# Four rearrangements in a hybrid recurrent layer: the gate rows, the way into the gated DeltaNet, the matrix memory's sample and the last products

## Chip, cores and metric

The kernel runs on one core of a Trainium2 chip. Its measure is the device time of one execution in microseconds.

## What is computed

One layer (D_MODEL = 1024) over a prompt of 1024 tokens and, at the same time, 8 sequences of 4 tokens each (the sample) that continue from given states. Three token mixers work on one input projection and are merged through gates; a feed-forward block and a final norm follow. The reference, cut:

```python
def mixer(xn, p, st):
    proj = jnp.einsum('btd,dc->btc', xn, p['w_in']).astype(f32)
    ...
    h, C1, n1, m1 = mlstm_scan(heads(ml_q), heads(ml_k) * HEAD_DIM ** -0.5, heads(ml_v), i_log, f_log, C0, n0, m0)
    ...
    conv = jax.nn.silu(sum(buf[:, j:j + t_len] * cw[j] for j in range(CONV_W)))
    o_gd, S1_gd = gdn_scan(l2n(heads(cq)) * HEAD_DIM ** -0.5, l2n(heads(ck)), heads(cv), beta, logg, S0_gd)
    y_gd = unheads(head_rms(o_gd) * p['gd_norm_w']) * jax.nn.silu(gd_z)
    ...
    o_hg, S1_hg = hgrn_scan(heads(jax.nn.silu(hg_q)), heads(k_hg), heads(hg_i), heads(jnp.log(g_f)), S0_hg)
    ...
    br = jnp.einsum('btnw,nwd->btnd', ys, p['w_branch'])
    merged = jnp.sum(gates * br, 2)
    return jnp.einsum('btd,de->bte', merged, p['w_out']), states

x = x + mixer(rmsnorm(x, norm1_w))
x = x + jnp.square(jax.nn.relu(rmsnorm(x, norm2_w) @ w_up)) @ w_down
y = rmsnorm(x, final_norm_w)
```

## The kernel before

All dense products (input projection, merge, output projection, feed-forward) have one form. A tile is 128 output columns over all T = 1056 tokens (1024 of the prompt, 32 of the sample), in three groups of 352 tokens (`TG`, `GN`). Each float32 operand is split in a high and a low part, and `dense` (line 415) makes three matmuls for each of the 8 pieces of the contraction: high by high, low by high, high by low. All of them have line 432 in the profile. Weights come through SyncE (`load_w`, line 384) into `w_raw`; ScalarE copies the high part (`make_hi`, `w_hi`, line 406), GpSimd subtracts it for the low part (`make_lo`, `w_lo`, line 412). Each group accumulates in one of two banks, `D0` and `D1`. ScalarE copies it out, into `u_in` for the columns of the short convolution (line 507) or into `stage` (line 451), from where it stores whole tiles to `proj` in memory (line 458). A group can begin only when ScalarE has emptied its bank.

The mixers' small operations lie between dense groups, in an order written out by hand. Each mixer's function is called once for each engine and calls `slot()` at fixed places. A `Filler` holds a list of weights, one for each slot, and puts that share of a run of tiles there: the dense pieces on TensorE, on ScalarE the weights' high parts and the copies of finished groups, on GpSimd the low parts. Each engine does its list strictly in order. On ScalarE and GpSimd a slot's work is held back until the next `slot()` or `slot.evacuate()`.

The four places, in order of time:

- **The gate rows** (`rows`, with the tiles 2 and 3 in its slots). The input and forget gates, decays and their running sums are made as rows of 36 x 128 by a long chain of small operations on VectorE, with exponentials on ScalarE and four tiny transposes on TensorE (`ends`, `prev`, `tok`). `tok` is the table with a column for each chunk.
- **The way into the gated DeltaNet.** After the convolutions GpSimd inverts small triangular blocks (`b_t`; VectorE turns them into `b_tt`). SyncE stores both to `td` (line 716) and loads them back in another shape as `d_t` and `d_tt` (line 1705). The chunk's product at line 1949 on TensorE needs all eight of these loads. `d_z` holds the output gate of a chunk; its columns are the last tiles before the loop (`stored_all(eng, GD0)` waits until they are in memory). `d_bc` are the four gate rows of a chunk, spread over all partitions; VectorE needs the next chunk's at the end of a chunk (`d_de`, line 1569), and ScalarE's four exponentials (line 1580) need that.
- **The matrix memory's sample** (`mlstm` with `sample`). Four heads read the states (line 2253), then come the denominators (2265, 2266), the sums of the keys (2270), the first of four state updates (`states("kv", h)`, line 872, two matmuls of 32 x 512), the transposes of `m_oc` (2276), and, with dense pieces between them, the other three updates.
- **The last products** (`last_down`): the down projection of the last block in three groups of 8 pieces of output `d`, the final norm's sum of squares (`SUM3`, shown as `f_sum`), and the scaling of finished columns (`SCALED` says which are scaled behind which piece).

Of the kernel before, what the change touches and what calls it, by code (L numbers as in the profile page):

```python
# [9 lines left out]
ALU = mybir.AluOpType  # L10
# [87 lines left out]
class Tile:  # L98
# [8 lines left out]
    @property  # L107
    def slot(self):
        return self.base % 2
# [15 lines left out]
def build(nc, xT, w_proj, w_half, w_full, par, con, rowpar, segrow, m0, conv0, st_ml, st_mn, st_gd, st_hg,  # L125
# [6 lines left out]
    with ExitStack() as ctx:  # L132
# [682 lines left out]
        hs_pool = steps("hs_pool", "gw" + DECAY_STEPS)  # L815
        GX_SLOTS, HS_SLOTS, MX_SLOTS = 15, 9, 10
        lb_dve, lb_act = steps("lb_dve", "d r n lb om"), steps("lb_act", "e ln")

        def pcols(tile, ntile, col, n):

            v = proj[tile:tile + ntile].rearrange("t p c -> p t c")
            return v[:, :, bass.ds(col, n)]
# [547 lines left out]
        def rows(kind, eng, slot):  # L1370
# [16 lines left out]
            if kind == "dve":  # L1387
# [38 lines left out]
                scan("loc", r_l[:, :], r_a[:, 1, :], r_in[:, 0, :], MASKED, ALU.add, ALU.max)  # L1426
                slot()

                eng.wait_ge(*rw_pe.after("ends"))
# [36 lines left out]
                slot()  # L1466
            if kind == "act":
                eng.wait_ge(*rw_dve.after("bc"))
                eng.activation(r_b[:, :, :], r_a[:, 0:2, :], ACT.Exp, scale=-1.0).then_inc(*rw_act.step("e"))
# [18 lines left out]
                eng.dma_start(s_m, r_mo[RP:RP + H, :]).then_inc(rw_mo, 16)  # L1488
                slot()
                eng.wait_ge(*rw_pe.after("tok"))  # L1490
                by_q = M[0][:, 0:5 * (RP + H)].rearrange("p (q x) -> p q x", q=5)
# [5 lines left out]
            if kind == "pool":  # L1497
                for _ in range(4):
                    slot()
            if kind == "pe":  # L1500
                slot()
                eng.wait_ge(*rw_dve.after("loc"))
                eng.transpose(M[1][0:1, 0:RP], r_a[0:RP, 0, last:CH], ident[0:RP, 0:RP])
                eng.transpose(M[1][0:1, RP:2 * RP], r_l[0:RP, last:CH], ident[0:RP, 0:RP]).then_inc(*rw_pe.step("ends"))
                slot()
                eng.wait_ge(*rw_dve.after("mp"))
                eng.transpose(M[2][0:RP, 0:1], r_c[0:1, 3 * RP:4 * RP], ident[0:1, 0:1]).then_inc(*rw_pe.step("prev"))
                slot()
                eng.wait_ge(*rw_dve.after("kd2"))
                eng.wait_ge(*rw_act.after("ex2"))  # L1510
                for q in range(5):
                    i = eng.transpose(M[0][:, q * (RP + H):(q + 1) * (RP + H)], r_tok[q], ident[0:RP + H, 0:RP + H])
                i.then_inc(*rw_pe.step("tok"))
                slot()
# [83 lines left out]
        def gdn(kind, eng, n, slot, sample, with_next=False, between=None):  # L1598
# [9 lines left out]
            def hn(x, o=0):  # L1608
                return x[:, o:o + C4].rearrange("p (h n) -> p h n", n=N)
# [48 lines left out]
            if kind == "sp":  # L1658
# [8 lines left out]
                if between != "rest":  # L1667
                    for k in range(2):
                        eng.dma_start(hn(B.qk, k * C4), pcols(GD_TILE + 4 * (1 - k), 4, col0, N)).then_inc(gx_in if sample else gd_in, 16)

# [5 lines left out]
                if n is None and not sample:  # L1676
# [3 lines left out]
                    for s_ in cv_st:  # L1680
                        eng.wait_ge(s_, 16 * NCONV // 2)
                eng.dma_start(hn(B.v), pcols(GD_TILE + 8, 4, col0, N)).then_inc(gx_in if sample else gd_in, 16)
                if n is not None or sample:
                    prefetch(eng, None if sample else n, (gd_dve, "ge"))
                    token_rows()

                def gates():
                    eng.dma_start(hn(B.z), pcols(GZ_TILE, 4, col0, N)).then_inc(gx_in if sample else gd_z, 16)

                if sample:  # L1690
                    gates()
                    eng.dma_start(flat_bh(d_Ss), of_state(st_gd)).then_inc(gxs_ld, 16)
                    return
                prefetch(eng, n, (gd_dve, "zs"))
                if n is not None:
                    gates()
                else:
                    inverse_loads(eng, 3)
                    eng.wait_ge(zeroed, 2)
                for w, x in enumerate((d_t0, d_tt0)):  # L1700
                    if n is None:
                        eng.wait_ge(iv_st[w], 16)
                    for a in range(NQ):
                        blocks = td[w, bass.ds(at, 1), :, a].rearrange("x h r c -> r (x h) c")
                        eng.dma_start(hn(x)[rows_of(a), :, rows_of(a)], blocks).then_inc(gd_t, 16)
                if n is None:
                    stored_all(eng, GD0)
                    gates()
                else:
                    slot()  # L1710
# [304 lines left out]
        def mlstm(kind, eng, n, slot, sample):  # L2015
# [164 lines left out]
            if kind == "act":  # L2180
# [19 lines left out]
                if sample:  # L2200
                    for _ in range(3):
                        slot()
                    eng.wait_ge(*pe_.after("num3"))
                    eng.activation(m_oc[:, :], M[0][0:N, :], ACT.Copy).then_inc(*act_.step("oc"))
                else:
                    slot.evacuate()
# [16 lines left out]
            if kind == "pe":  # L2223
# [40 lines left out]
                if sample:  # L2264
# [3 lines left out]
                    for h in range(H):  # L2268
                        at = 2 * C4 + h * DEC_BATCH
                        i = eng.matmul(M[1][:, at:at + DEC_BATCH], tk(m_kt, h), cst[0:NS, CC_IND:CC_IND + DEC_BATCH],  # L2270
                                       start=True, stop=True)
                    i.then_inc(*pe_.step("kn"))
                    states("kv", 0)
                    eng.wait_ge(*act_.after("oc"))
# [25 lines left out]
        GROUPS = [(g, d) for g in range(TG) for d in range(KT)]  # L2300
        SCALED = {3: (0,), 4: (1, 2), 5: (3, 4), 6: (5, 6), 7: (7,)}
        nm_act = {"3": steps("nm3_act", " ".join(f"q{g}{d}" + (f" l{g - 1} r{g - 1}" if g and d == 1 else "") for g, d in GROUPS) + f" l{TG - 1} r{TG - 1}")}
# [469 lines left out]
        def last_down(kind, eng):  # L2772
# [4 lines left out]
            def cols(g):  # L2777
                return slice(g * GN, (g + 1) * GN)
# [21 lines left out]
            for g, d in GROUPS if kind != "pool" else ():  # L2800
# [23 lines left out]
                if kind == "dve":  # L2824
                    eng.wait_ge(groups_done, n + 1)
                    eng.tensor_tensor(acc[:, d, cols(g)], acc[:, d, cols(g)], bank, ALU.add).then_inc(bank_free[n % 2], 1)
                    if d:
                        eng.wait_ge(*act_.after(f"q{g}{d - 1}"))
                        if d == 1:
                            eng.tensor_copy(SUM3[:, cols(g)], SQ3[0][:, cols(g)]).then_inc(*dve_.step(f"a{g}0"))  # L2830
                        else:
                            eng.wait_ge(*dve_.after(f"a{g}{d - 2}"))
                            eng.tensor_tensor(SUM3[:, cols(g)], SUM3[:, cols(g)], SQ3[(d - 1) % 2][:, cols(g)], ALU.add).then_inc(*dve_.step(f"a{g}{d - 1}"))
                    for k in SCALED.get(d, ()) if g else ():
                        scale(g - 1, k)
# [14 lines left out]
        def flat_bh(x):  # L2850
# [4 lines left out]
        LOOP_GD, LOOP_HG, LOOP_ML = GD0, GD0 + 19, GD0 + 38  # L2855
        ROW_SLOTS, ML_SLOTS = [9, 2, 4, 3], [3, 3, 3, 3, 3, 3]
        HG_SLOTS = [3, 1, 2, 3, 3, 3, 3]
# [6 lines left out]
                  ("hg", hgrn, LOOP_HG, HG_SLOTS, [9, 5, 5, 5, 5, 5, 7, 7, 24], 3),  # L2864
                  ("ml", mlstm, LOOP_ML, ML_SLOTS, [5, 5, 4, 4, 4, 4, 4, 5, 5, 8], 2))

# [100 lines left out]
        def _(sp):  # L2967
# [60 lines left out]
            gdn("sp", sp, None, None, False, between="rest")  # L3028
            chunk_loads(sp, gdn, LOOP_GD, 0, 3)
            rest_of_conv()  # L3030
# [254 lines left out]
```

## Time and profile before

| | |
|---|---|
| median of 3 runs | 2195.5 us |
| lowest, highest | 2195.11, 2198.4 us |
| the profiled execution | 2200.46 us, of which the span is 2198.7 |
| mean granted clock of TensorE | 0.995 |
| TensorE busy | 2166.3 us (99%) |
| VectorE, ScalarE, GpSimd busy | 44%, 34%, 26% |
| instructions | 36263 |

The times are those of whole executions; the profile is another execution, and the span runs from its first to its last instruction. Times in the profile count from the span's start. A granted clock of 1.00 is TensorE's upper level, 2.4 GHz, and 0.50 the lower, 1.2 GHz. A busy TensorE is not one at its peak, since ends of matmuls are modelled.

### The profile page before, as it was taken

How to read it: one execution, taken by the hardware profiler on the slowest of the kernel's cores; microseconds unless marked ns; L12 is line 12 of the kernel's file. 1: busy time of each engine (PE TensorE's matmuls, PEld its weight loads, DVE VectorE, ACT ScalarE, POOL GpSimd, SP SyncE). 2: the span in 40 equal slices, each digit the busy share in tenths (PEclk: the TensorE clock that was granted, in tenths of full speed). 3: DMA queues.
4: the chain of work that ended last, by engine and by line, in shares of the span. 5: the costliest groups of instructions: out<-in, count | busy, mean ns of one | idle time of the engine just before them, and what ended most of it. 6: DMA issues, size and time to landing. Idle time of an engine off the chain costs nothing.

```text
span 2198.7 us, 36263 instructions
## 1 busy us (share of the span) xinstructions
PE 2166.3 (99%) x13762; PEld 2104.9 (96%) x13762; DVE 971.9 (44%) x1522; ACT 758.2 (34%) x1342; POOL 571.2 (26%) x375
## 2 busy tenths in 40 slices
PE   7999999999999999999999999999999999999998
PEld 6999999999899999899998999999999999999997
DVE  5888323333665664244445365442222222222225
ACT  5556323232465563233332333231312213122132
POOL 2438623323211212212212222212221221212120
PEclk9999999999999999999999999999999999999999
DMA  4224536442244323456431744202111111111112
GB/s 173 67 80 135 162 114 188 128 133 89 83 125 144 99 97 118 128 161 193 143 109 59 254 148 146 97 25 58 29 58 34 52 52 33 57 33 52 52 40 88
DMA packets 191538, 222.09 MB, mean 101 GB/s; under 512 B 38670, under 2 KB 146226, under 8 KB 191334
## 3 DMA queue, kind: packets, MB, share of 16 engines
q1 hardware_dynamic: 164364, 179.81, 27.0%
q10 hardware_dynamic: 27098, 41.23, 5.3%
q8 instruction: 53, 0.87, 0.2%
q14 instruction: 23, 0.19, 0.0%
HBM read 162.22 MB, written 58.77 MB: 101 GB/s over the span
## 4 chain that ended last, share of the span: by engine, by line
PE 79%; issue 8%; POOL 4%; DVE 4%; DMA 2%; ACT 2%; SPq 1%; ACTq 0%; POOLq 0%; DVEq 0%
PE D L432 65%; PE D L2811 2%; POOL w_lo L412 2%; POOL b_t L738 1%; POOL b_u L735 1%; DVE u_x L546 1%; PE MM L1302 1%; PE MM L1890 1%; DMA proj<-stage 0%; PE MM L2367 0%; PE MB L1974 0%; PE MM L872 0%; PE MB L2284 0%; PE D L2367 0%; PE MB L2234 0%
## 5 line engine op out<-in xcount | busy, mean ns | idle before, releaser
L432 PE MATMUL D<-xn_hi,w_hi 128*128 128x352 f32 x1992 | 663.7, 333 | 7.3 <-ACT stage L451 2.8
L412 POOL TENSOR_TENSOR w_lo<-w_raw,w_hi 128x1024 fp32r<-128x1024 f32 (+1 forms) x163 | 338.7, 2078 | 1184.7 <-ACT w_hi L406 1184.7
L432 PE MATMUL D<-xn_lo,w_hi 128*128 128x352 f32 x1992 | 644.2, 323 | 0.0
L432 PE MATMUL D<-xn_hi,w_lo 128*128 128x352 f32 x1992 | 643.9, 323 | 0.0
L432 PEld LDWEIGHTS D<-xn_hi,w_hi 128*128 128x128 f32 x1992 | 375.7, 189 | 22.5 <-issue 12.8
L432 PEld LDWEIGHTS D<-xn_lo,w_hi 128*128 128x128 f32 x1992 | 375.8, 189 | 4.7 <-issue 3.8
L432 PEld LDWEIGHTS D<-xn_hi,w_lo 128*128 128x128 f32 x1992 | 375.5, 189 | 0.0
L406 ACT ACTIVATE w_hi<-w_raw 128x1024 fp32r<-128x1024 f32 (+1 forms) x163 | 143.7, 882 | 346.8 <-PE D L432 296.4
L432 PE MATMUL D<-z_lo,w_hi 128*128 128x352 f32 x768 | 247.9, 323 | 0.0
L432 PE MATMUL D<-z_hi,w_lo 128*128 128x352 f32 x768 | 247.8, 323 | 0.0
L432 PE MATMUL D<-z_hi,w_hi 128*128 128x352 f32 x768 | 247.2, 322 | 0.0
L432 PE MATMUL D<-h_lo,w_hi 128*128 128x352 f32 x672 | 217.1, 323 | 0.0
L432 PE MATMUL D<-h_hi,w_lo 128*128 128x352 f32 x672 | 216.6, 322 | 0.0
L432 PE MATMUL D<-h_hi,w_hi 128*128 128x352 f32 x672 | 216.5, 322 | 0.0
L2748 DVE TENSOR_TENSOR acc<-acc,D 128x352 f32<-128x352 f32 x168 | 87.5, 521 | 225.0 <-PE D L432 225.0
L451 ACT ACTIVATE stage<-D 128x352 f32<-128x352 f32 x177 | 80.8, 457 | 239.8 <-PE D L432 223.5
L432 PEld LDWEIGHTS D<-z_hi,w_hi 128*128 128x128 f32 x768 | 144.2, 188 | 0.1
L432 PEld LDWEIGHTS D<-z_hi,w_lo 128*128 128x128 f32 x768 | 144.3, 188 | 0.0
L432 PEld LDWEIGHTS D<-z_lo,w_hi 128*128 128x128 f32 x768 | 144.2, 188 | 0.1
L2734 ACT ACTIVATE f_v<-f_u 128x352 f32<-128x352 f32 x96 | 47.8, 498 | 246.2 <-DVE f_u L2741 246.2
L432 PEld LDWEIGHTS D<-h_hi,w_hi 128*128 128x128 f32 x672 | 126.3, 188 | 0.0
L432 PEld LDWEIGHTS D<-h_hi,w_lo 128*128 128x128 f32 x672 | 126.2, 188 | 0.0
(557 smaller groups left out, 3066.6 us busy)
## 6 DMA issues: line engine op xcount, KB each, us to landing
w_raw<-in_w_proj SPq DMA_DIRECT2D x73, 512.0 KB, 3.7
proj<-stage ACTq DMA_DIRECT2D x60, 528.0 KB, 3.3
w_raw<-in_w_half SPq DMA_DIRECT2D x72, 256.0 KB, 2.7
w_raw<-in_w_full SPq DMA_DIRECT2D x24, 512.0 KB, 3.6
stage<-proj SPq DMA_DIRECT2D x23, 528.0 KB, 3.6
d_bc<-rowd SPq DMA_DIRECT2D x32, 256.0 KB, 5.7
m_in<-proj SPq DMA_DIRECT2D x32, 256.0 KB, 3.8
f_w<-in_w_full SPq DMA_DIRECT2D x16, 512.0 KB, 3.5
```

The costliest lines, as they stand in the source:

```text
L406: nc.scalar.activation(w_hi[t.slot][:, 0:kt, :], buf[:, 0:kt * P].rearrange("p (k m) -> p k m", m=P), ACT.Copy).then_inc(w_hi_made, 1)
L412: nc.gpsimd.tensor_tensor(w_lo[t.slot][:, 0:kt, :], raw(t)[0][:, 0:kt * P].rearrange("p (k m) -> p k m", m=P), w_hi[t.slot][:, 0:kt, :].bi ...
L432: last = nc.tensor.matmul(D[b][:, 0:GN], w[t.slot][:, k, :], x, start=(k == 0 and n == 0), stop=(k == kt - 1 and n == 2))
L451: nc.scalar.activation(stage[:, t.slot, g * GN:(g + 1) * GN], D[t.bank(g)][:, 0:GN], ACT.Copy).then_inc(bank_free[t.bank(g)], 1)
L546: eng.scalar_tensor_tensor(x, conv_in(c)[:, j + 1:j + 1 + CONV_LEN], tap(j + 1), x, ALU.mult, ALU.add).then_inc(*cv_dve.step(f"{now}{c}"))
L735: pool.tensor_tensor(part, b_a[:, k + 1:BLK, k:k + 1].to_broadcast([P, n, k + 1]), b_t[:, k, 0:k + 1].unsqueeze(1).to_broadcast([P, n, k + ...
L738: pool.tensor_tensor(b_t[:, k + 1:BLK, 0:k + 1], b_t[:, k + 1:BLK, 0:k + 1], part, ALU.subtract).then_inc(*iv_pool.step(f"t{k}"))
L1302: i = eng.matmul(level(j, slice(0, N))[:, h * (N // 2):(h + 1) * (N // 2)], hn(g_kl, j * N4)[:, h, :], g_ql[:, j * HF + h * (N // 2):j * H ...
L1890: i = eng.matmul(MM[0:N, h * 2 * N:(h + 1) * 2 * N].rearrange("p (x n) -> p x n", n=N), hn(B.qk, C4)[:, h, :], q_and_k, start=True, stop=True)
L2734: eng.activation(v, u, ACT.Square).then_inc(f_sq, 1)
L2748: eng.tensor_tensor(acc[:, m - FT, cols], acc[:, m - FT, cols], D[t.bank(g)][:, 0:GN], ALU.add).then_inc(bank_free[t.bank(g)], 1)
L2811: last = eng.matmul(bank, w[:, k, :], x[:, k, cols(g)], start=(k == 0 and j == 0), stop=(k == FT - 1 and j == 2))
```

## The change

It adds and removes no arithmetic and no transfer. The diff, cut to what matters:

```diff
@@ rows
             if kind == "act":
+                slot()
+                slot.evacuate()
                 eng.wait_ge(*rw_dve.after("bc"))
...
                 slot()
+                slot.evacuate()
                 eng.wait_ge(*rw_pe.after("tok"))
...
-        ROW_SLOTS, ML_SLOTS = [9, 2, 4, 3], [3, 3, 3, 3, 3, 3]
+        ROW_SLOTS, ML_SLOTS = [3, 6, 2, 4, 3], [3, 3, 3, 3, 3, 3]
@@ gdn, SyncE's part
                 if between != "rest":
-                    for k in range(2):
-                        eng.dma_start(hn(B.qk, k * C4), pcols(...)).then_inc(...)
+                    if between != "ahead":
+                        for k in range(2):
+                            eng.dma_start(hn(B.qk, k * C4), pcols(...)).then_inc(...)
...
-                eng.dma_start(hn(B.v), pcols(GD_TILE + 8, 4, col0, N)).then_inc(...)
-                if n is not None or sample:
+                if between != "ahead":
+                    eng.dma_start(hn(B.v), pcols(GD_TILE + 8, 4, col0, N)).then_inc(...)
+                if (n is not None or sample) and between != "behind":
                     prefetch(eng, None if sample else n, (gd_dve, "ge"))
                     token_rows()
...
                 else:
+                    stored_all(eng, GD0)
+                    gates()
                     inverse_loads(eng, 3)
...
-                if n is None:
-                    stored_all(eng, GD0)
-                    gates()
-                else:
+                if n is not None:
                     slot()
@@ the SyncE program
             gdn("sp", sp, None, None, False, between="rest")
-            chunk_loads(sp, gdn, LOOP_GD, 0, 3)
+            gdn("sp", sp, 0, None, False, between="ahead")
+            load_w(sp, Tile(LOOP_GD + 2), w_proj[LOOP_GD + 2])
+            gdn("sp", sp, 0, lambda: load_w(sp, Tile(LOOP_GD + 3), w_proj[LOOP_GD + 3]), False, between="behind")
+            chunk_loads(sp, gdn, LOOP_GD, 1, 3)
@@ mlstm, the sample
                     eng.activation(m_oc[:, :], M[0][0:N, :], ACT.Copy).then_inc(*act_.step("oc"))
+                    slot()
...
                     i.then_inc(*pe_.step("kn"))
+                    slot()
                     states("kv", 0)
...
-                  ("ml", mlstm, LOOP_ML, ML_SLOTS, [5, 5, 4, 4, 4, 4, 4, 5, 5, 8], 2))
+                  ("ml", mlstm, LOOP_ML, ML_SLOTS, [5, 5, 4, 4, 4, 3, 4, 4, 5, 5, 5], 2))
@@ last_down
-        SCALED = {3: (0,), 4: (1, 2), 5: (3, 4), 6: (5, 6), 7: (7,)}
+        SCALED = {3: (0,), 4: (1, 2), 5: (3, 4), 6: (5,), 7: (6, 7)}
...
-                    eng.wait_ge(groups_done, n + 1)
-                    eng.tensor_tensor(acc[:, d, cols(g)], acc[:, d, cols(g)], bank, ALU.add).then_inc(bank_free[n % 2], 1)
+                    def gather():
+                        eng.wait_ge(groups_done, n + 1)
+                        eng.tensor_tensor(acc[:, d, cols(g)], acc[:, d, cols(g)], bank, ALU.add).then_inc(bank_free[n % 2], 1)
+
+                    if d < KT - 1:
+                        gather()
                     if d:
...
+                    if d == KT - 1:
+                        gather()
                     for k in SCALED.get(d, ()) if g else ():
                         scale(g - 1, k)
```

In `rows` the added slots hold 3 + 6 pieces where one held 9, so TensorE's order there stays. ScalarE's queue in the gate rows, from the store of tile 1 on, before (`r_...` are the row operations):

```order
L2349 DMA proj<-stage 128x1056
L1469 ACTIVATE r_row<-r_a 36x256
L1471 ACTIVATE r_a<-r_row 36x256
L1472 ACTIVATE r_par<-r_par 36x1
L1473 ACTIVATE r_a<-r_a 36x128
L1475 ACTIVATE r_a<-r_a 36x128
L1477 ACTIVATE r_row<-r_a 36x128
L406 ACTIVATE w_hi<-w_raw 128x1024
L507 ACTIVATE u_in<-D 128x352 x2
```

and now:

```order
L2359 DMA proj<-stage 128x1056
L406 ACTIVATE w_hi<-w_raw 128x1024
L507 ACTIVATE u_in<-D 128x352
L1472 ACTIVATE r_row<-r_a 36x256
L1474 ACTIVATE r_a<-r_row 36x256
L1475 ACTIVATE r_par<-r_par 36x1
L1476 ACTIVATE r_a<-r_a 36x128
L1478 ACTIVATE r_a<-r_a 36x128
L1480 ACTIVATE r_row<-r_a 36x128
L507 ACTIVATE u_in<-D 128x352
```

The weights' high part and the first of the two `u_in` copies have passed ahead of the six row operations.

SyncE's queue from the last load of `d_v` ahead of the loop, before (behind it the loop's own issues begin: weights, `d_qk`, `d_v`, `d_bc`):

```order
L1682 DMA d_v<-proj 128x4x128
L716 DMA td<-b_t 128x1024
L716 DMA td<-b_tt 128x1024
L1705 DMA d_t<-td 32x4x32 x4
L1705 DMA d_tt<-td 32x4x32 x4
L1688 DMA d_z<-proj 128x4x128
```

and now:

```order
L1689 DMA d_v<-proj 128x4x128
L1695 DMA d_z<-proj 128x4x128
L716 DMA td<-b_t 128x1024
L716 DMA td<-b_tt 128x1024
L1716 DMA d_t<-td 32x4x32 x4
L1716 DMA d_tt<-td 32x4x32 x4
L1680 DMA d_bc<-rowd 128x4x128 x4
L384 DMA w_raw<-in_w_proj 128x1024
L1675 DMA d_qk<-proj 128x4x128 x2
L1689 DMA d_v<-proj 128x4x128
```

`d_z` (with the wait of `stored_all`) stands ahead of the two `td` stores, and the next chunk's `d_bc` ahead of its weights, `d_qk` and `d_v`.

TensorE in the matrix memory's sample, from the sums of the keys, before (`D<-` are dense matmuls):

```order
L2270 MATMUL MB<-cst,m_kt 128x8 x4
L872 MATMUL MM<-m_vx,m_kt 128x512
L872 MATMUL M<-m_vx,m_kt 128x512
L2276 MATMUL MB<-cst,m_oc 128x32 x4
L432 MATMUL D<-xn_hi,w_hi 128x352
L432 MATMUL D<-xn_lo,w_hi 128x352
L432 MATMUL D<-xn_hi,w_lo 128x352
```

and now:

```order
L2279 MATMUL MB<-cst,m_kt 128x8 x4
L432 MATMUL D<-xn_hi,w_hi 128x352
L432 MATMUL D<-xn_lo,w_hi 128x352
L432 MATMUL D<-xn_hi,w_lo 128x352
L432 MATMUL D<-xn_hi,w_hi 128x352
L432 MATMUL D<-xn_lo,w_hi 128x352
L432 MATMUL D<-xn_hi,w_lo 128x352
L432 MATMUL D<-xn_hi,w_hi 128x352
L432 MATMUL D<-xn_lo,w_hi 128x352
L432 MATMUL D<-xn_hi,w_lo 128x352
L872 MATMUL MM<-m_vx,m_kt 128x512
L872 MATMUL M<-m_vx,m_kt 128x512
```

Nine dense matmuls stand ahead of the first update. The sample's last slot holds nine fewer.

## Rows read from the trace of the kernel before

**Rows 1.** The page, part 4: the chain that ended last, shares by engine
```profile
PE 79%; issue 8%; POOL 4%; DVE 4%; DMA 2%; ACT 2%; SPq 1%; ACTq 0%; POOLq 0%; DVEq 0%
```

**Rows 2.** TensorE's waits over the whole span: total, times, longest
```profile
PE D L432 <- ACT stage L451: 2.8, 1, 2.8
PE D L432 <- ACT u_in L507: 2.4, 2, 1.6
```

**Rows 3.** Windows: length, engines busy (instructions), granted clock, DMA share, GB/s
```profile
271.80:278.60 6.80, 5.48 (x20) 5.48 (x21) 0.69 (x1) 1.61 (x6) 0.73 (x1) 0.50 0.47 160
1186.60:1193.40 6.80, 6.80 (x23) 5.06 (x21) 3.05 (x7) 0.31 (x1) 0.00 (x0) 0.50 0.00 0
```

**Rows 4.** Timeline of ScalarE around the gate rows: start, duration
```profile
58.99 0.79 ACT L507 ACTIVATE u_in<-D 128x352 f32<-128x352 f32 x2
...
72.98 0.56 ACT L1493 ACTIVATE tok<-MB 128x32 f32<-128x32 f32 x5
73.43 0.84 ACT L507 ACTIVATE u_in<-D 128x352 f32<-128x352 f32 x2
```

**Rows 5.** Timeline of GpSimd inside the inversion
```profile
178.89 3.45 POOL L412 TENSOR_TENSOR w_lo<-w_raw,w_hi 128x1024 fp32r<-128x1024 f32 x1 [1.42 <-ACT w_hi L406]
```

**Rows 6.** Timeline of SyncE's DMA issues before the first chunk
```profile
249.40 0.34 SPq L716 DMA_DIRECT2D td<-b_t  x1
...
252.12 2.49 SPq L1705 DMA_DIRECT2D d_t<-td  x4
254.70 1.81 SPq L1705 DMA_DIRECT2D d_tt<-td  x4
...
259.94 4.00 SPq L1674 DMA_DIRECT2D d_bc<-rowd  x4
```

**Rows 7.** Timeline of VectorE, the next chunk's decay
```profile
270.71 0.69 DVE L1569 TENSOR_TENSOR d_de<-d_bc,cst 128x512 f32<-128x512 f32 x1 [4.64 <-DMA d_bc<-rowd]
```

**Rows 8.** TensorE's timeline at 257.91, then the chain: start, us
```profile
257.91 0.48 PE L1949 MATMUL MB<-d_t,d_mt 128*128 128x128 f32 x2
...
263.31 7.38 DMA d_bc<-rowd
...
273.12 4.77 PE D L432 x15
...
279.20 2.39 PE D L432 x15
```

**Rows 9.** Tile stage in 240 to 258: ScalarE's store
```profile
L458 ACTq DMA_DIRECT2D proj<-stage x1: 338/338/338, 250.6 to 250.6; - x1
...
DMA to landing us min/median/max: 2.8/2.8/2.8
```

**Rows 10.** DMA issues, 236 to 285, 250 to 258: KB, us to landing
```profile
td<-b_t SPq DMA_DIRECT2D x1, 512.0 KB, 2.7
...
d_tt<-td SPq DMA_DIRECT2D x4, 16.0 KB, 1.7
```

**Rows 11.** Windows of line 432 alone: PE, PEld busy, clock, DMA share
```profile
893.40:897.60 4.20, 0.00 (x0) 0.00 (x0) 1.00 0.32 129
1182.20:1189.30 7.10, 0.00 (x0) 0.00 (x0) 0.81 0.00 0
```

**Rows 12.** The chain through the matrix memory's sample
```profile
1186.08 1.27 PE MM L872 x2
1187.35 1.71 PE M L872 x2
...
1189.43 3.82 PE D L432 x12
...
1196.59 0.86 PE MB L872 x2
```

**Rows 13.** Timelines of VectorE and TensorE at the last group
```profile
2188.01 0.52 DVE L2826 TENSOR_TENSOR acc<-acc,D 128x352 f32<-128x352 f32 x1
...
2189.27 0.53 PE L2789 MATMUL MM<-f_sum,cst 128*128 128x352 f32 x1 [1.29 <-ACT f_q L2821]
```

More of the change, by code:

```diff
@@ L815, in build @@
         hs_pool = steps("hs_pool", "gw" + DECAY_STEPS)
-        GX_SLOTS, HS_SLOTS, MX_SLOTS = 15, 9, 10
+        GX_SLOTS, HS_SLOTS, MX_SLOTS = 15, 9, 11
         lb_dve, lb_act = steps("lb_dve", "d r n lb om"), steps("lb_act", "e ln")
@@ L1497, in rows @@
             if kind == "pool":
-                for _ in range(4):
+                for _ in range(5):
                     slot()
             if kind == "pe":
+                slot()
                 slot()
@@ L1667, in gdn @@
                 if between != "rest":
-                    for k in range(2):
-                        eng.dma_start(hn(B.qk, k * C4), pcols(GD_TILE + 4 * (1 - k), 4, col0, N)).then_inc(gx_in if sample else gd_in, 16)
+                    if between != "ahead":
+                        for k in range(2):
+                            eng.dma_start(hn(B.qk, k * C4), pcols(GD_TILE + 4 * (1 - k), 4, col0, N)).then_inc(gx_in if sample else gd_in, 16)
                 def token_rows():
@@ L1681, in gdn @@
                         eng.wait_ge(s_, 16 * NCONV // 2)
-                eng.dma_start(hn(B.v), pcols(GD_TILE + 8, 4, col0, N)).then_inc(gx_in if sample else gd_in, 16)
-                if n is not None or sample:
+                if between != "ahead":
+                    eng.dma_start(hn(B.v), pcols(GD_TILE + 8, 4, col0, N)).then_inc(gx_in if sample else gd_in, 16)
+                if (n is not None or sample) and between != "behind":
                     prefetch(eng, None if sample else n, (gd_dve, "ge"))
@@ L1688, in gates @@
                     eng.dma_start(hn(B.z), pcols(GZ_TILE, 4, col0, N)).then_inc(gx_in if sample else gd_z, 16)
+                if between == "ahead":
+                    return
                 if sample:
@@ L2204, in mlstm @@
                     eng.activation(m_oc[:, :], M[0][0:N, :], ACT.Copy).then_inc(*act_.step("oc"))
+                    slot()
                 else:
@@ L2272, in mlstm @@
                     i.then_inc(*pe_.step("kn"))
+                    slot()
                     states("kv", 0)
```

## The prediction

> **What bounds the kernel now.** I read the chain that ended last first: 79% of the span is TensorE at work, and only small shares belong to anything else [rows 1]. So what is to be found is where TensorE waits, and where it runs at its lower clock. TensorE's waits are few: 2.8 us once for an evacuation into `stage`, and 2.4 us in two pieces (0.8 and 1.6) for `u_in` [rows 2]. Then the granted clock in windows: it stands at 1.00, the 2.4 GHz level, nearly everywhere, and at 0.50, the 1.2 GHz level, in 271.8 to 278.6 and in 1186.6 to 1193.4 [rows 3]. The four edits touch these four places and the tail. A change of 0.2% (4.4 us) is about what a measurement of this kernel can tell from none.
>
> The sum is made against the profiled execution, 2200.46 us with a span of 2198.7. The median of the three timed runs is 2195.5, 5.0 us less, and those runs differ by 3.3 us among themselves, about the size of one clock dip below. The sum of changes is carried over to the median.
>
> **The gate rows (48 to 76 us).** TensorE's stream keeps its order; ScalarE's changes. Before, ScalarE sits in front of the first exponential of the row work, then does six small activations, then the high part of the next weights, and only at 58.99 the copy that frees TensorE's bank [rows 4]; TensorE has waited 0.8 us for it [rows 2]. The copy now goes ahead of the exponentials, so that wait goes. The exponentials wait for VectorE's inputs anyway, so the row chain isn't later. Its later links hang on TensorE's transposes, which come some 0.8 earlier. At the second place the five `tok` copies stand ahead of the freeing copy, 72.98 against 73.43 [rows 4]; they now stand behind it. The freeing copy starts at 72.98 - 0.8 = 72.2 instead of 73.43, 1.25 us sooner, and TensorE's place is that much earlier. I take **-1.3 us**, bounds -0.8 (only the first) and -2.4 (both waits whole). What is delayed against it is `tok`, by the 0.84 of the two copies. The gain must pass GpSimd's long inversion, which ends just before 249.40. Its order is unchanged, and at 178.89 it waits 1.42 us for ScalarE's weights [rows 5], which TensorE paces, so it moves along. If it didn't, this term would be 0.
>
> **Into the gated DeltaNet (242 to 280 us), SyncE's queue.** Before, SyncE issues the store of `b_t` at 249.40, the first `d_t` load at 252.12, `d_tt` at 254.70, and much later, from 259.94 on, the next chunk's `d_bc` [rows 6]. The last of these lands at 270.7, 7.38 after its issue [rows 8], and VectorE has been idle 4.64 us for it [rows 7]. Behind VectorE stands ScalarE's `d_de`, behind that the copy that frees the bank, behind that TensorE: the 2.8 us wait [rows 2] that ends at 273.12, and the low clock. The fifteen dense records after it take 4.77 us against 2.39 for the next fifteen [rows 8], a loss of 2.4.
>
> Two edits answer this. The four `d_bc` loads (256 KB each) pass ahead of the weights, `d_qk` and `d_v` in the queue; and the load of `d_z`, a 0.4 us issue, moves from behind the eight `d_t`/`d_tt` loads to ahead of the stores that these read. I look at the second more closely. `d_z` is read from tiles that ScalarE has just stored, and the move takes the wait for those stores with it. The last was issued at 250.6 and took 2.8 us to land [rows 9]. SyncE therefore stands until 253.4. Queued behind it: the two `td` stores, then eight loads. The store of `b_t` goes out at 253.4 + 0.4 + 0.1 = 253.9 instead of 249.40, 4.5 us later, and 2.7 for its landing, 2.49 and 1.81 for the issues and 1.7 for the last landing follow as before [rows 6, 10]. Who waits for it: the product at line 1949, which needs all eight. It ran at 257.91 [rows 8]; the last of the four `d_tt` issues, at 0.45 each, began at about 256.1 and landed 1.7 later, at 257.8. So there is no slack. The product comes 4.4 us late, with TensorE idle.
>
> From below: the eight issues at 0.34 each, as the big stores have [rows 6], end the last landing at 256.6 + 2.4 + 1.7 = 260.7, 2.9 late. From above: one microsecond more for each of the two landings, since the 256 KB of `d_z` now run ahead of the store, 6.4. I take 4.4, the durations of the same instructions.
>
> After that stall everything on TensorE is 4.4 later, and `d_bc` can't hold it any more. SyncE is through with `d_tt` at 253.9 + 2.7 + 2.49 + 1.81 + 0.1 = 261.0; the last `d_bc` issue comes 3.4 later, as before, and even at the old 7.38 lands at 271.8. From landing to TensorE's start it was 2.4 us, so 274.2; TensorE asks at 273.1 - 2.8 + 4.4 = 274.7. So the old 2.8 goes whole. The low clock doesn't: the idle stretch is longer than the one that brought it, so I leave its 2.4 as it was (1.2 to 3.4 are possible). Sum **4.4 - 2.8 = +1.6 us**, bounds -1.1 (2.9 - 2.8 - 1.2) and +4.6 (6.4 - 2.8 + 1.0). An earlier `d_z` gains nothing itself: none of TensorE's waits hangs on it [rows 2].
>
> The Trainium skill (DMA: Bandwidth & Descriptors, the section on the anatomy of one DMA) gives about 2.0 us fixed for each DMA plus the bytes. By it the store would take 3.2 and the last small load 2.0 where the rows have 2.7 and 1.7, and the stall would be longer by about 0.5.
>
> **The matrix memory's sample (1166 to 1210 us).** Nine dense matmuls move from the end of the sample to between the keys' sums (line 2270) and the first state update. In 1182.2 to 1189.3 there is no dense record at all, at a mean clock of 0.81; the clock falls at 1186.6 [rows 3, 11]. The price is in the chain: twelve dense records in 3.82 at the low clock, where fifteen take 2.39 at the high one, so twelve 1.91 [rows 8, 12]; the second half of the update 1.71 against 0.86 a head later [rows 12]; and some 0.2 in its first half: 3.0 us. With the nine in place the stretches without dense work are 1182.1 to the update's start at 1186.1 [rows 12], and then the update and the transposes, about 2.3 us at full clock. Is 4.0 us short enough? HGRN2's sample has 4.2 us without a dense record in 893.4 to 897.6, of the same kinds of products, and keeps 1.00 [rows 11]. So I take the dip as gone. The nine at full clock cost what they cost at the end, nothing. What hides behind the nine: the update and the transposes of `m_oc` start 1.4 later, and VectorE's `m_h` with them; twelve dense records (1.9 us) still stand between them and the sum of squares. But the next stage's loads hang on VectorE's last state addition, which gains 1.4 less than TensorE; I give back 0.5 there (0 to 1.4). **-2.5 us**, bounds 0 and -3.4.
>
> The Trainium skill (TensorE: Matmul & The Clock Gate, on HAM oscillation) counts a dip as half of the throttled time. That would make 3.4 of each 6.8 us dip, where the rows have 3.0 and 2.4; by it the sum below would be 0.4 lower.
>
> **The last products (2141 to 2199 us).** VectorE adds the running sum before the eighth group instead of behind it, and one scaling moves one group later. VectorE picks the last group up at 2188.01; TensorE's next start is 2189.27, and what it waited 1.29 us for is ScalarE's square, not the running sum [rows 13]. The square hangs on the group's own addition, which can't come before the group. **0**, bounds -0.5 and +0.1.
>
> **Sum:** -1.3 + 1.6 - 2.5 + 0 = -2.2 us, 2198.3 for the profiled execution and 2195.5 - 2.2 = **2193.3** at the median.
>
> **The rivals.**
> 1. *The dip in the sample stays*, since 4.0 us with the 8-column products is weaker work than HGRN2's. Then -1.3 + 1.6 = +0.3: 2195.8.
> 2. *No new stall in the DeltaNet*: the stored tiles land sooner, or the product at 1949 has slack that I don't see. Then the old wait and its dip go: -1.3 - 2.8 - 2.4 - 2.5 = -9.0: 2186.5. For it speaks that `d_bc` is plainly what VectorE waits for; against it, the issue times, which leave 0.1 us of slack.
> 3. *Slower*: the loads of `d_t` and `d_tt`, now in the same burst as `d_z`, take what `d_bc` took, 7.4 us instead of 1.7 [rows 8, 10]. The stall becomes 4.4 + 5.7 = 10.1, the term 7.3, and with the sample's dip kept the whole is -1.3 + 7.3 = +6.0: 2201.5. It decides from a landing of about 5.8 us (+4.4). Against it: they are 16 KB loads and SyncE issues nothing behind them until they are out.
>
> **How the numbers follow.** My forecast 0.55, rival 1 0.2, rival 2 0.12, rival 3 0.05, and 0.08 for values between the forecast and rival 2. The range reaches to rival 1's upper side (three runs scatter by 3.3) and part of the way to rival 2: 2188.5 to 2199. Faster than 2191.1 are rival 2 and most of what lies between: 0.2. Slower than 2199.9 is rival 3: 0.05. The rest, 0.75, is within 0.2%.
>
> **What would show it.** Gate rows: no wait of TensorE near 59, about 1.1 left near 72. DeltaNet: SyncE's store of `b_t` near 252.6 (253.9 less the 1.3), a new idle of some 4 us on TensorE ahead of line 1949's product, released by `d_tt`'s load, and none before the next tile; the granted clock still falls there. Sample: clock 1.00 throughout 1180 to 1195. Tail: unchanged. The prediction is wrong if TensorE doesn't wait for `d_tt`, or if a dip stands where none did.

## The result and the profile after

The changed kernel takes 2199.98 us at the median (2198.19 to 2202.32, 20 runs), the kernel before, run beside it, 2196.64 (2193.69 to 2201.1, 20 runs): ratio 1.0017, 95% interval 1.0011 to 1.0023. It is 3.3 us slower, where 2.2 us faster was forecast. Its profiled execution took 2202.32 us with a span of 2200.4; that of the kernel before 2200.46 with 2198.7. So the two traces differ by 1.7 us where the medians differ by 3.3, and that difference turns out to matter. The ratios and intervals here and below are those on record, not quotients of the two medians; the two can differ by up to 0.0008 (1.8 us).

What TensorE waited for in the changed kernel (the view of waits: engine, tile and line, what it waited for; us in total, times, longest). Against [rows 2]:

```profile
PE MB L1957 <- DMA d_tt<-td: 5.3, 1, 5.3
...
PE D L432 <- DVE acc L2652: 1.5, 3, 0.9
...
PE MM L2799 <- ACT f_q L2831: 1.3, 1, 1.3
...
PE D L432 <- ACT u_in L507: 1.1, 1, 1.1
```

The wait of 2.8 us for `stage` is gone, and so is one of the two for `u_in`; the one for `f_q` is as it was. New are 5.3 us at line 1957, the product that stood at 1949, and 1.5 us for VectorE's `acc` in the merge of the halves, near 1220 us.

SyncE's queue in the same trace (start, us, line, tiles, how many), against [rows 6]:

```profile
252.12 0.38 SPq L1695 DMA_DIRECT2D d_z<-proj  x1
252.55 0.51 SPq L716 DMA_DIRECT2D td<-b_t  x1
253.11 0.42 SPq L716 DMA_DIRECT2D td<-b_tt  x1
256.87 1.76 SPq L1716 DMA_DIRECT2D d_t<-td  x4
258.68 1.85 SPq L1716 DMA_DIRECT2D d_tt<-td  x4
260.64 2.04 SPq L1680 DMA_DIRECT2D d_bc<-rowd  x4
```

and the chain of what ended last there (start, us, what), against [rows 8 to 10]:

```profile
249.46 2.64 DMA proj<-stage
252.12 0.38 SPq L1695
...
252.55 4.25 DMA td<-b_t
...
260.10 1.77 DMA d_tt<-td
261.87 0.12 issue
261.99 2.07 PE MB L1957 x8
264.06 4.35 PE D L432 x15
268.40 0.84 PE MM L1962 x8
```

Read it from the top: SyncE stands for ScalarE's last store of `proj`, lets `d_z` go, and only then stores `b_t`, at 252.55 where I had written "near 252.6". But that store takes 4.25 us to land instead of 2.7. The four `d_t` issues then take 1.76 us instead of 2.49, which gives some of it back, and TensorE stands idle for 5.27 us ahead of the product. The windows (stretch, its length, busy time and count of PE, PEld, DVE, ACT and POOL, then TensorE's granted clock, DMA share and GB/s) show the low clock behind it, and a second low stretch, in HGRN2's sample, where the trace before has none. The matrix memory's sample has full clock:

```profile
262.00:264.00 2.00, 2.00 (x9) 2.00 (x10) 0.00 (x0) 0.00 (x0) 0.00 (x0) 0.50 0.60 82
...
900.00:902.00 2.00, 2.00 (x8) 2.00 (x8) 1.63 (x2) 0.00 (x0) 0.00 (x0) 0.50 0.00 0
...
1180.00:1195.00 15.00, 15.00 (x97) 12.22 (x96) 11.03 (x14) 2.12 (x5) 5.60 (x3) 1.00 0.01 4
```

### The profile page after: what moved, and what is told of

It is laid out like the page before. It is cut to its first block, busy times and chain, and to the rows that moved or that the text cites. A ratio compares the mean times of both kernels' runs of the same rounds, so it can differ in the third digit from the quotient of the medians.

```text
span 2200.4 us, 36222 instructions
## 1 busy us (share of the span) xinstructions
PE 2164.9 (98%) x13762; PEld 2104.1 (96%) x13762; DVE 968.9 (44%) x1522; ACT 757.9 (34%) x1342; POOL 571.5 (26%) x375
## 4 chain that ended last, share of the span: by engine, by line
PE 81%; issue 10%; DVE 3%; DMA 2%; ACT 1%; POOL 1%; SPq 0%; ACTq 0%; POOLq 0%; DVEq 0%
PE D L432 68%; PE D L2821 2%; POOL w_lo L412 1%; PE MM L1898 1%; DMA w_raw<-in_w_half 1%; DVE u_x L546 0%; PE MB L1957 0%; PE MB L1982 0%; PE MM L872 0%; PE MB L2294 0%; PE D L2377 0%; PE MM L1964 0%; PE MB L2243 0%; PE MB L2262 0%; PE MM L1323 0%
```

## Experiments: the parts one by one

The first four kernels each make one part of the change alone. The question is whether the 5.5 us between forecast and result lie in `d_z`'s move (theory A), in the early `d_bc` (B) or in the sample (C). Each kernel is compared with the kernel before, run in the same group as it.

**The gate rows alone.** `ROW_SLOTS`, the two `slot.evacuate()` calls and the added slots of the change.

```diff
-        ROW_SLOTS, ML_SLOTS = [9, 2, 4, 3], [3, 3, 3, 3, 3, 3]
+        ROW_SLOTS, ML_SLOTS = [3, 6, 2, 4, 3], [3, 3, 3, 3, 3, 3]
...
             if kind == "act":
+                slot()
+                slot.evacuate()
...
```

> The kernel before with the gate rows' edits alone (ROW_SLOTS, the two evacuations of ScalarE, the added slots). Both theories of the miss leave this term as predicted: the trace after has TensorE 1.58 us nearer behind 74 us than ahead of 59 us, so about -1.6 us, within -0.8 and -2.4. If GpSimd's long inversion or the wait for the stored rows swallows it, 0. A median above that of the kernel before by 1 us or more would make this term the failed one.

Measured: 2195.0 against 2196.85, ratio 0.9991 (0.9982 to 1.0). The size is as expected, -1.85 us, at the edge of what the interval can tell.

**`d_bc` ahead, `d_z` left where it was.** The conditions on `between` for `d_qk`, `d_v` and `d_bc` are those of the change.

```diff
-            chunk_loads(sp, gdn, LOOP_GD, 0, 3)
+            gdn("sp", sp, 0, None, False, between="ahead")
+            load_w(sp, Tile(LOOP_GD + 2), w_proj[LOOP_GD + 2])
+            gdn("sp", sp, 0, lambda: load_w(sp, Tile(LOOP_GD + 3), w_proj[LOOP_GD + 3]), False, between="behind")
+            chunk_loads(sp, gdn, LOOP_GD, 1, 3)
```

> The kernel before with the four d_bc loads alone moved ahead of the weights, d_qk and d_v; d_z stays behind the d_t and d_tt loads. Theory A (all the loss in the DeltaNet is the move of d_z, and the miss is that this stall was sized too small while the old stall's low clock is often absent anyway): no new stall, the wait of 2.8 us for ScalarE near 270 goes, and up to 2.4 us of low clock with it: -2.8 to -5.2 us. Theory B (the four 1 MB of d_bc ahead of the weights delay the weights' loads, and part of the loss comes from there): the wait comes back at the next weights, -1 to +1 us.

Measured: 2197.09, ratio 1.0 (0.9991 to 1.0009), +0.24 us. Theory A's number failed: taking away the 2.8 us wait and its low clock, as I thought, is worth nothing. The number is B's, but not B's mechanism, since the trace shows no new wait for the next weights. (The four loads of `d_bc` are 256 KB each, 1 MB in all, not "four 1 MB".) The chain shows the last `d_bc` issued at 258.7, not 263.3 [rows 8], and landing

```profile
258.76 9.21 DMA d_bc<-rowd
268.00 0.70 DVE d_de L1569
...
270.40 2.67 PE D L432 x15
```

9.21 us later instead of 7.38: part of the lead is lost in the landing. And a wait of 2.8 us for it to remove isn't there in most executions, as the repeated profiles below show, only one of about 1.0. That one is gone in this trace, which is too little for the medians; and the trace of the kernel with `d_z` put back, below, has `d_bc` just as early, a landing of 9.67 us and a wait of 0.5 us left, as long as in the kernel that has the gate rows' and the sample's edits and `d_bc` in its old place.

**`d_z` moved, `d_bc` left where it was.**

```diff
                 if n is not None:
                     gates()
                 else:
+                    stored_all(eng, GD0)
+                    gates()
                     inverse_loads(eng, 3)
```

and the same two calls taken out behind the `d_t` and `d_tt` loads.

> The kernel before with the load of d_z and its wait for the stores alone moved ahead of the td stores. Theory A: the product at line 1957 of the changed kernel comes 5.3 us late as in the trace after, SyncE's later issues all shift with it, so the old wait for d_bc stays behind it: +5 us, near 2201.6. Rival: with d_z out of its burst d_bc lands in 5 us instead of 7.4 and the new stall swallows the old one: +2.5 us.

Measured: 2203.02 (6 runs), ratio 1.0032 (1.002 to 1.0044), +6.2 us. Theory A holds for the stall and is one microsecond short in size. Its second half failed: no wait for ScalarE is left behind the stall. The rival was right that the new stall swallows the old wait, though the last `d_bc` load takes 6.5 us to land and not its 5. The profiled execution (2199.16) is the fastest of the six, and has full clock in the matrix memory's sample. TensorE's wait and the landings in this kernel's chain:

```profile
PE MB L1948 <- DMA d_tt<-td: 4.8, 1, 4.8
```

```profile
250.71 2.64 DMA proj<-stage
...
253.80 4.00 DMA td<-b_t
...
261.10 1.66 DMA d_tt<-td
```

**The matrix memory's sample alone.**

```diff
-        GX_SLOTS, HS_SLOTS, MX_SLOTS = 15, 9, 10
+        GX_SLOTS, HS_SLOTS, MX_SLOTS = 15, 9, 11
...
                     eng.activation(m_oc[:, :], M[0][0:N, :], ACT.Copy).then_inc(*act_.step("oc"))
+                    slot()
...
                     i.then_inc(*pe_.step("kn"))
+                    slot()
                     states("kv", 0)
...
-                  ("ml", mlstm, LOOP_ML, ML_SLOTS, [5, 5, 4, 4, 4, 4, 4, 5, 5, 8], 2))
+                  ("ml", mlstm, LOOP_ML, ML_SLOTS, [5, 5, 4, 4, 4, 3, 4, 4, 5, 5, 5], 2))
```

> The kernel before with the matrix memory's sample alone changed (nine dense records between the keys' sums and the first state update, weights of the slots). Theory A: a small gain, the profile's 3.0 us of low clock less 1.3 us of later waits in the merge, -1 to -2 us. Theory C (the low clock only moves: in the trace after HGRN2's sample has a stretch at 0.50 that the trace before hasn't, and the merge's waits stay): 0 to +2 us, and the trace shows a stretch of low clock elsewhere.

Measured: 2195.91, ratio 0.9995 (0.9986 to 1.0004), -0.94 us. That is the small gain of A, not told apart from none. The low clock in the sample does go: the mean granted clock of all 11 runs is 0.998 or 0.999, where only 7 of the 28 runs of the kernel before beside them reach 0.998. The four parts sum to -1.85 + 0.24 + 6.17 - 0.94 = +3.6 us, against +3.3 for the whole change.

## Experiments: what in the move of `d_z` costs, and was the old wait always there?

**The whole change with `d_z` put back.** Every other edit stays; `stored_all` and `gates()` stand behind the eight loads again.

> The changed kernel with the load of d_z and its wait put back behind the d_t and d_tt loads; all its other edits stay (rows, d_bc ahead, the sample's nine records, the last products). Measured alone, the parts gave -1.85 (rows), +0.24 (d_bc) and -0.94 us (sample). Theory A (the parts add up, and d_z's place alone makes the changed kernel slower): -2.5 us against the kernel before, 2194.3, and some 6 us below the changed one. Rival: with d_bc's burst earlier the parts disturb one another, as the changed kernel's DeltaNet did: not below the kernel before.

Measured: 2194.32 against 2197.25, ratio 0.9984 (0.9975 to 0.9993), -2.9 us. Theory A, and faster than both kernels. `d_z`'s place (the wait with the load) alone turns the change from a gain into a loss.

**The wait alone in the new place.** The load of `d_z` stays behind.

```diff
                 else:
+                    stored_all(eng, GD0)
                     inverse_loads(eng, 3)
```

> The kernel before with only the wait for ScalarE's last proj stores put ahead of the td stores; the load of d_z itself stays behind the d_t and d_tt loads. Theory W (SyncE stands at that wait, and this is most of the cost): the store of b_t goes out 3.9 us late as in the run with d_z moved (253.37 against 249.40), lands in 2.7 us, the product is 3.9 us late, and with the low clock behind it the kernel is +4 to +5.5 us. Theory L (the 256 KB of d_z ahead of the store is what costs, the stores having landed by then anyway): 0 to +2 us.

Measured: 2201.2, ratio 1.0018 (1.0009 to 1.0027), +3.95 us; TensorE's wait is 3.3 us. Theory W for the greater part: wait and loss come out just under its 3.9 and +4 to +5.5, and the four `d_t` issues take 1.78 us where the kernel before has 2.49. Its chain has the store landing as it did before, in 2.63 us:

```profile
250.65 2.65 DMA proj<-stage
...
253.32 2.63 DMA td<-b_t
...
259.27 1.91 DMA d_tt<-td
```

With the 256 KB load of `d_z` in front of it the same store took 4.00 and 4.25 us. So the load is what lengthens TensorE's wait from 3.3 to 4.8: 0.4 of issue (253.37 to 253.80) and 1.4 of landing, less 0.25 that the last landing is shorter. Between the medians, which come from different groups, it is 2.2 (6.17 less 3.95); the other 0.7 is low clock or scatter. The stretch at 0.50 behind the stall is 3.4 us long here and 6.8 with the load moved too.

**Wait and load between the stores and the loads.** `stored_all` and `gates()` behind `inverse_loads(eng, 3)` instead of ahead of it.

> The kernel before with the wait and the load of d_z between the td stores and the d_t loads. The td stores go out as before and land during the wait. By theory W SyncE is free at about 253.4 plus 0.4, 1.7 us later than the 252.12 of the kernel before: the product waits some 1.7 us, +1.7 to +3.5 us. By theory L the load of d_z stands ahead of the eight loads and delays them as it did the store: +4 us or more.

Measured: 2196.42, ratio 1.0004 (0.9995 to 1.0013): no difference that can be told, below what was expected. Theory L is out as the main cause. W's direction holds in the trace, with a wait of 1.1 us for `d_tt`; but behind it the wait for `stage` is 0.2 instead of 1.0, so the new wait only takes the old one's place:

```profile
PE MB L1948 <- DMA d_tt<-td: 1.1, 1, 1.1
...
PE D L432 <- ACT stage L451: 0.2, 1, 0.2
```

**The kernel before, profiled again, twice.**

> The kernel before, unchanged, a second profiled execution. If the wait for ScalarE near 270 (d_bc landing 7.38 us after its issue) and its low clock belong to every execution, they stand in it again: a wait of some 2.8 us and a stretch at 0.50 near 272 to 278. If they came by chance with a late landing, as the two executions with the same SyncE order (landing in 6.59 and 6.10 us, no low clock there) suggest, they are absent or short and the span is nearer 2195 than 2198.7.

> The kernel before, a third profiled execution. If the wait of 2.8 us near 270 and its low clock are rare, as five of six executions with this order of SyncE's queue say, there is again a wait of at most 1.4 us there and clock 1.00; if they are common, they may stand in it again.

The second one's sentence miscounts: four executions with this order of SyncE's queue had been profiled by then, three of them without the low clock, not "five of six".

Measured: spans 2195.6 and 2196.8, with one run each of 2197.38 and 2198.57 us. In the first, TensorE's wait and the landing are

```profile
PE D L432 <- ACT stage L451: 1.0, 1, 1.0
```

```profile
263.50 6.04 DMA d_bc<-rowd
```

and its windows, over the stretch where [rows 3] have 0.50:

```profile
270.00:274.00 4.00, 3.00 (x22) 2.86 (x21) 1.36 (x3) 1.98 (x6) 1.39 (x1) 1.00 0.38 44
274.00:278.00 4.00, 4.00 (x30) 4.00 (x29) 0.00 (x0) 1.91 (x3) 0.80 (x1) 1.00 0.65 252
```

The wait is 1.0 us, not 2.8, and the clock stays up. The second repeat has 0.9. With the kernels that leave SyncE's queue alone, seven executions of this order are on hand: waits of 2.8, 1.0, 0.9, 1.0, 1.0, 1.4 and 0.5 us, landings of 7.38 us in the first and 5.78 to 6.59 in the others, and a low clock near 272 in the first alone. The timed runs say the same with more of them. The execution that I predicted from has a mean granted clock of 0.995. Of the 78 timed runs of the kernel before in the three groups of experiments none is that low, and of the 12 with the last products' edit alone one is (0.995, 2203.6 us). The execution that I predicted from was the odd one.

**The changed kernel, profiled again.**

> The changed kernel, a second profiled execution. What belongs to every execution stands in it again: the idle of about 5.3 us ahead of line 1957's product, the low clock behind it, clock 1.00 in the matrix memory's sample and the later waits in the merge. The low clock in HGRN2's sample at 900 to 903 was in one of ten executions here and should be absent; without it the span is about 2198.8.

Measured: span 2198.0. The wait at 1957 is back with 5.1 us (the store of `b_t` landing in 4.21), the low clock behind it too (0.57 over 260 to 268); HGRN2's sample is at full clock. As expected. Of the changed kernel's 20 timed runs five have a mean clock of 0.995, as its first profile has; eleven have 0.997, as the second.

**Rows and sample only; last products only.** The first has the gate rows' and the sample's edits and nothing else, the second

```diff
-        SCALED = {3: (0,), 4: (1, 2), 5: (3, 4), 6: (5, 6), 7: (7,)}
+        SCALED = {3: (0,), 4: (1, 2), 5: (3, 4), 6: (5,), 7: (6, 7)}
```

with VectorE's addition of the running sum ahead of the last group's.

> The kernel before with the gate rows' and the matrix memory sample's edits; SyncE's queue and the last products as before. Measured alone they gave -1.85 and -0.94 us: -2.8 us, near 2194.3, and level with the version that has d_bc ahead and the last products' edit too (2194.32), if those two are worth nothing. If d_bc ahead is worth the 1.0 to 1.7 us that the profiled executions show around 270 us, this kernel is 1 us or more above 2194.3.

> The kernel before with the last products' edit alone. Predicted 0, bounds -0.5 and +0.1; the changed kernel's profile agrees (the wait for f_q is 1.3 us in both). Rival: the last addition now stands behind the square's sum on VectorE and the tail loses some tenths: +0.3 us.

Measured: 2194.34 against 2198.52, ratio 0.9989 (0.998 to 0.9998). The version that has `d_bc` ahead was at 2194.32 in another group, with ratio 0.9984 (0.9975 to 0.9993): the intervals overlap widely. The last products alone: 2198.1, ratio 1.0 (0.999 to 1.001). The early `d_bc` and the last products are worth nothing that can be measured.

## Where the time went, execution by execution

TensorE runs the same matmuls in all these kernels, so the start of each record can be set against that of the same record in the first repeat of the kernel before. The table gives by how much the lead or lag (median over the records of a stretch) changed from 30-48 to 80-240 us (gate rows), to 290-530 (DeltaNet), from 560-860 to 910-1100 (HGRN2's sample), and from 1110-1160 to 1250-1500 (matrix memory's sample and merge). "low" marks a stretch of low clock there.

```
kernel                     gate rows  DeltaNet   HGRN2     sample+merge
before (predicted from)      -0.4     +4.2 low   -0.2       0.0 low
before again                  0        0          0         0   low
before again, 2              +1.5 low -0.2        0.0      -0.1 low
last products alone          -0.1      0.0        0.0      -3.1
rows alone                   -2.0     -0.2       +0.2      -1.5 low
sample alone                 +1.7 low +0.3       -0.2      -1.1
rows and sample              -2.0     -0.5       +1.6 low  -1.8
d_bc ahead                   -0.4     -1.0       +1.0      +0.8 low
d_z put back                 -2.0     -0.6       -0.1      -1.4
d_z between                  +1.2 low +0.1       -0.3      +0.4 low
wait alone                   -0.5     +3.5 low   -0.2      +0.2 low
d_z moved                    -0.4     +5.4 low   +0.1      -3.4
changed                      -1.9     +6.7 low   +1.6 low  -1.3
changed again                -1.9     +6.3 low    0.0      -1.5
```

In the DeltaNet the changed kernel loses 6.3 to 6.7 us against a usual execution of the kernel before: the 5.3 us wait, less the usual 1.0, and 2.4 of low clock behind it (5.27 - 1.0 + 2.4 = 6.7; the 2.4 is what is left of the 6.7). The records show the 2.4: the first eight take 2.07 us where they take 1.15 at full clock, the fifteen dense ones 4.35 where 2.4 is usual; that is 2.9 by their durations, which overlap a little. Against the one odd execution the same loss reads as 2.5. So read, the two first profiles give -1.5 in the gate rows, +2.5 in the DeltaNet, +1.8 in HGRN2's sample and -1.3 in the matrix memory's: +1.5 of their 1.7 us.

## Why the prediction was wrong

**Gate rows: right.** -1.3 forecast, -1.4 to -2.0 between executions that have no low clock there (-1.9 to -2.0 against -0.5 to 0), -1.85 at the median. Both waits went as said: none near 59, 1.12 left at 72.8, and the inversion moved along, with `td`'s stores. The median gains more, perhaps because three of the nine executions with the old order have a stretch of low clock at 74 to 80 us that costs 1.5 to 2, and none of the five with the new one has. All three are among the four of those nine that have no low clock near 26 us; two of the five with the new order have none there either, and none at 74. That this is the edit's doing, and not chance, isn't shown.

**DeltaNet: this is the step that failed.** The mechanism of the new stall was right to the record: SyncE stands for the `proj` stores, the store of `b_t` goes out at 252.55, TensorE idles ahead of the product, `d_tt` releases it, and the low clock follows. Two sizes were wrong. First, "I take 4.4, the durations of the same instructions": it was 5.27, because the store landed in 4.25 us and not in 2.7 behind `d_z`'s load. The upper bound had foreseen that for both landings; only the first took longer (1.4 to 1.6 us), the second 1.7 as ever. And 2.49 for the four `d_t` issues was too much: in all four executions with the wait ahead of the stores they take 1.76 to 1.78. So 4.4 + 1.55 - 0.7 is the 5.3, and the second miss covers part of the first.

The Trainium skill (DMA: Bandwidth & Descriptors, the section on the anatomy of one DMA) gives its 2.0 us and the bytes for the path of GpSimd, while this store is SyncE's. Its estimate of 3.2 for the store stands between the 2.63 that it took alone and the 4.25 here, and its 2.0 is above the 1.66 to 1.91 of the last small load. Put in place of 2.7 and 1.7 they add 0.8, not the "about 0.5" of the prediction, and give 5.2; that this is near 5.3 is luck, since the store is still 1.05 short in it and the issues 0.7 too long.

Second, and larger: "So the old 2.8 goes whole" and, of the low clock, "so I leave its 2.4 as it was". That set a saving of 2.8 and a low clock that was there already against the new stall. The old wait does go; it is its size that was wrong. In six of seven executions the old wait is 0.5 to 1.4 us and brings no low clock. The true term was 5.3 - 1.0 + 2.4 = +6.7, where I had 4.4 - 2.8 + 0 = +1.6. The sum was made against an execution of 2200.46 us and then carried to a median of 2195.5 unchanged. Those 5 us between them were to be seen, and the DeltaNet's 4.2 us in the first row above are most of them. The rest is that three runs were few: 20 runs of the same kernel have their median at 2196.64.

That isn't all of the miss. Against the odd execution too the change measures +1.7 and not -2.2: 0.9 more for the new stall (5.27, not 4.4), 1.8 for a low clock in HGRN2's sample that no edit touches, 1.2 less gained in the matrix memory's sample. The prediction's reading of the whole trace was short as well, without harm here: it left out a wait of 9.7 us for `nsq` and a stretch of 3.4 us at 0.50, both in the first 30 us.

**The sample: the direction right, the size less.** -2.5 forecast; -0.94 at the median, and in the table a mean of -1.4 over five executions with the new order against -0.7 over nine with the old. The low clock does go: none of five has it, seven of nine old ones have. But two of the old ones run without it too, and those (-3.1 and -3.4) are faster than any with the edit. For the nine records delay what follows. Timelines of TensorE and VectorE, the keys' sums and the last addition to the state, first in the changed kernel:

```profile
1188.12 1.05 PE L2279 MATMUL MB<-cst,m_kt 32*128 32x8 f32 x8
1208.82 0.68 DVE L864 TENSOR_TENSOR m_Cs<-m_Cs,MB 128x512 f32<-128x512 f32 x1
```

and in the kernel with the last products' edit alone, which has the old order here and no low clock:

```profile
1181.84 1.05 PE L2270 MATMUL MB<-cst,m_kt 32*128 32x8 f32 x8
1200.84 0.68 DVE L864 TENSOR_TENSOR m_Cs<-m_Cs,MB 128x512 f32<-128x512 f32 x1
```

From start to start that is 20.7 us, as in all five executions with the edit, against 19.0. In the old order they are 22.1 to 22.2 with the usual 6.8 us of low clock (six executions), 20.5 with half of that (one) and 19.0 without (two). So the addition comes 1.4 to 1.5 us sooner than behind a low clock and 1.7 later than without one. The next stage's loads hang on it, and TensorE waits 1.2 to 1.6 us for `acc` where executions with the old order have between nothing and 1.1. I had given back 0.5 for that, "0 to 1.4", where it is the upper end that holds; and the low clock that the edit takes away is absent in some executions anyway. That the clock would stay up was forecast rightly: the stretch without a dense record is 4.26 us with the edit, and the clock stays at 1.00 in all five.

The Trainium skill (TensorE: Matmul & The Clock Gate, on HAM oscillation) counts half of the throttled time as lost. For stretches of some 6.8 us that is 3.4. Here they cost 2.4 (DeltaNet) to 3.4 (the sample, by the two executions without one), so it is at the upper end.

**Last products: right.** The wait for `f_q` is 1.3 us with and without the edit, and the edit alone measures ratio 1.0.

**The sum.** -1.85 (rows), +6.5 in the DeltaNet (the mean of the two) less 0.5 (the mean of the seven executions with the old queue), -0.94 (sample) and 0: +3.2, against +3.3 measured. That they agree to a tenth is luck, since each median is uncertain by a microsecond or two.

## What to carry to other kernels

A profiled execution that is 5 us above the median carries stalls that most executions don't have; before a wait of a few microseconds is counted as a saving, look for it in a second profile, above all if a DMA's landing ends it. A load put ahead of a store in the same queue brings its own wait along for everything behind it, so ask first who waits for what stands there, and try the place behind the stores: here it cost nothing that could be measured, where the place ahead of them cost 6 us. When a stall is removed and another made, compare both in usual executions, since their low clock isn't a constant either.

## What the hardware showed that I had not expected

- The low clock isn't fixed by the program. With the order of before it stood in the matrix memory's sample in seven of nine executions, at 74 to 80 us in three of nine, and in HGRN2's sample, untouched by any edit, in two of fourteen. In the DeltaNet it came each time behind a long wait for `d_tt` or `stage`: 2.8, 3.3, 4.8, 5.1 and 5.3 us; never there behind those of 1.4 us and less.
- A DMA's landing depends on its neighbours in the queue. The store of `b_t` took 2.63 us behind the wait alone and 4.00 to 4.25 with a 256 KB load issued just ahead of it, everything else equal. The last `d_bc` load took 5.78 to 7.38 us behind the weights, `d_qk` and `d_v`, but 9.21 and 9.67 when issued ahead of them, 3 to 5 us sooner; which of its new neighbours holds it up was not tested.
